# One transformer step on one core: the chunk inverse of the delta rule computed by another recurrence, in all four quarters of the array

## The reference, cut to what matters

```python
kb = kc * bc[..., None]
L = jnp.where(strict, jnp.einsum('nbhid,nbhjd->nbhij', kb, kc) * decay, 0.0)
rhs = jnp.concatenate([vc * bc[..., None], kb * jnp.exp(gc)[..., None]], axis=-1)
sol = lax.linalg.triangular_solve(eye + L, rhs, left_side=True, lower=True, unit_diagonal=True)
```

## Time and profile before

| | us |
|---|---|
| median of 3 runs | 1689.42 |
| profiled execution, whole | 1689.16 |
| its span (what the page's shares refer to) | 1687.2 |
| PE busy | 1665.5 (99%) |
| DVE busy | 1049.7 (62%) |
| ACT busy | 738.7 (44%) |
| POOL busy | 188.5 (11%) |
| part of the span in which the two inverses run | 69 to 107 and 161 to 202 |

### The profile page before, as it was taken

How to read it: one execution, slowest core, us unless ns; L and a number is a source line. 1 busy time by engine, 2 the same in 40 slices (tenths; PEclk the granted TensorE clock), 3 DMA queues, 4 the chain that set the end, 5 groups by cost and what they waited for, 6 DMA issues and landing times.

```text
span 1687.2 us, 23136 instructions
## 1 busy us (share of the span) xinstructions
PE 1665.5 (99%) x9357; PEld 1403.4 (83%) x9357; DVE 1049.7 (62%) x1567; ACT 738.7 (44%) x1137; POOL 188.5 (11%) x170
## 2 busy tenths in 40 slices
PE   9999999999999999999999999999999999999998
PEld 7787897987898888888988888888898888888887
DVE  7889798474489349549675643655574545354445
ACT  6654477553553223223542323323364645253462
POOL 0455470300300000000100000000100000000001
PEclk9999999999999999999999999999999999999999
DMA  6112134421223323323322213213212222222221
GB/s 218 60 44 63 52 106 132 139 75 51 78 73 113 102 73 118 104 78 100 119 88 81 100 51 106 100 60 110 76 66 79 72 78 86 75 88 75 87 75 51
DMA packets 45576, 147.67 MB, mean 88 GB/s; under 512 B 5024, under 2 KB 8992, under 8 KB 45472
## 3 DMA queue, kind: packets, MB, share of 16 engines
q1 hardware_dynamic: 45472, 146.21, 26.3%
HBM read 144.09 MB, written 2.10 MB: 87 GB/s over the span
## 4 chain that ended last, share of the span: by engine, by line
PE 84%; DVE 11%; ACT 2%; issue 2%; POOL 0%; DVEq 0%; ACTq 0%; POOLq 0%
PE ps L507 21%; PE ps L509 21%; PE ps L508 21%; PE ps L512 20%; DVE sl L2054 2%; DVE ps L2271 1%; DVE ps L2114 1%; DVE y L2478 1%; DVE xl L2495 1%; DVE ps L2108 0%; ACT sh L1307 0%; DVE h L2488 0%; DVE pad L2106 0%; PE ps L1128 0%; DVE ss L2232 0%
## 5 line engine op out<-in xcount | busy, mean ns | idle before, releaser
L1307 ACT ACTIVATE sh<-raw 128x1024 fp32r<-128x1024 f32 x257 | 268.2, 1053 | 372.8 <-PE ps L509 256.7
L2054 DVE TENSOR_TENSOR sl<-raw,sh 128x1024 fp32r<-128x1024 f32 x257 | 321.7, 1259 | 131.5 <-ACT sh L1307 131.4
L507 PE MATMUL ps<-xh,sh 128*128 128x512 f32 (+1 forms) x664 | 262.9, 396 | 0.0
L509 PE MATMUL ps<-xl,sh 128*128 128x512 f32 (+1 forms) x664 | 253.9, 382 | 0.0
L508 PE MATMUL ps<-xh,sl 128*128 128x512 f32 (+1 forms) x664 | 253.8, 382 | 0.0
L507 PE MATMUL ps<-sh,xh 128*128 128x512 f32 x384 | 151.8, 395 | 0.0
L509 PE MATMUL ps<-sl,xh 128*128 128x512 f32 x384 | 149.7, 390 | 0.0
L508 PE MATMUL ps<-sh,xl 128*128 128x512 f32 x384 | 149.7, 390 | 0.0
L509 PEld LDWEIGHTS ps<-xl,sh 128*128 128x128 f32 x664 | 124.8, 188 | 24.9
L507 PEld LDWEIGHTS ps<-xh,sh 128*128 128x128 f32 x664 | 124.9, 188 | 24.5 <-issue 0.7
L508 PEld LDWEIGHTS ps<-xh,sl 128*128 128x128 f32 x664 | 125.1, 188 | 22.7 <-issue 0.7
(11 more groups left out here) (438 smaller groups left out, 3320.4 us busy)
## 6 DMA issues: line engine op xcount, KB each, us to landing
raw<-in_wup SPq DMA_DIRECT2D x44, 512.0 KB, 3.5
raw<-in_wdn SPq DMA_DIRECT2D x24, 512.0 KB, 3.5
raw<-in_rqk SPq DMA_DIRECT2D x16, 512.0 KB, 3.6
raw<-in_rv SPq DMA_DIRECT2D x16, 512.0 KB, 3.4
raw<-in_rg SPq DMA_DIRECT2D x16, 512.0 KB, 4.3
raw<-in_rout SPq DMA_DIRECT2D x16, 512.0 KB, 3.5
raw<-in_sv SPq DMA_DIRECT2D x16, 512.0 KB, 3.4
raw<-in_sg SPq DMA_DIRECT2D x16, 512.0 KB, 3.5
```

Source lines behind the costliest of these rows:

```text
L507: e.matmul(dst, wh, ah, start=start, stop=False, skip_group_check=True)
L509: return e.matmul(dst, wh, al, start=False, stop=stop, skip_group_check=True)
L1307: e.activation(SH[j % NSPL][:], RAW[j % NRAW][:], ACT.Copy).then_inc(*hi(j))
L2054: e.tensor_tensor(SL[j % NSPL][:], RAW[j % NRAW][:], SH[j % NSPL][:].bitcast(F32), ALU.subtract).then_inc(*lo(j))
```

## The change

The inverse is computed by another recurrence. With L' = L plus 2I (`UL` is changed in place), D starts as L' and Z as the masked transpose (mask e1). At each of six levels there are two products: "dt" = UT^T Z, which DVE multiplies by the next mask (e2, e4, ... e32; each is half the identity minus one block pattern) to give the next Z, and "d" = Z^T UT, which ACT copies to the next `UT`. At the last level only dt is made, and DVE subtracts the identity while it writes `UTF`. So there are 1 + 5x2 + 1 = 12 products of 16 matmuls where there were 1 + 5 + 5 + 4 = 15. The POOL masks, the DVE copies L2198 and the operation `UX` are gone.

Each product now writes two banks, one per head. For head 0 of the pair a matmul goes from partitions R to the same R; for head 1 it goes to the other half (R and RO swap from level to level). Four matmuls in a row (two heads, two parities) so lie in four different 64x64 quarters. dt goes to banks 6 and 7 in both chains, d to the chain's own two. Chain 0 makes a level in one beat, so everything behind it (keys, u, w, recurrence) comes 4 beats earlier; chain 1 keeps two beats for levels 0 to 3 and one for levels 4 and 5, so its later steps stay in their beats.

The eight PSUM tensors become one of 4096 columns, of which `PS[i]` are views. The diff, cut to its core:

```diff
-CSH = ["id64", "mc", "ms", "m1t", "m2t", "m4t", "m8t", "m16t", "m32t"]
+CSH = ["id64", "mc", "ms", "e1", "e2", "e4", "e8", "e16", "e32"]
...
+        def heads(p, i):
+
+            b = 6 if i else KBANK[p][0]
+            return PSUM[:, b * 512:b * 512 + 1024].rearrange("p (h q b c) -> p h q b c", h=2, q=2, c=64)[:, :, 0]
...
# tensor_program, chain(p)
-                pe.wait_ge(*gdv[(p, "tt", 0)])
+                pe.wait_ge(*gdv[(p, "d1t")])
                 for h, tb, par in CHUNKS:
                     o = (h * 4 + tb) * 64
                     R = RR[par]
-                    t = one(b[R, o:o + 64], UTT[p][R, o:o + 64], csh["id64"][R, :], True, True)
...
-                for n_ in range(5):
...
+                    t = one(b[R, o:o + 64], UL[p][R, o:o + 64], csh["id64"][R, :], True, True)
+                t.then_inc(*gmm((p, "d", 0)))
+                rel[A_] = [(gac, (p, "d", 0))]
+                yield
+                for n_ in range(6):
+                    Z = UZ[p][n_ % 2]
+                    pe.wait_ge(*gac[(p, "d", n_)])
+                    pe.wait_ge(*gdv[(p, "z", n_)])
+                    for lhs, rhs, i in ((UT[p], Z, 1), (Z, UT[p], 0))[:2 if n_ < 5 else 1]:
+                        two = (6, 7) if i else KBANK[p]
+                        b2 = [bank(k) for k in two]
+                        for tb, h, par in product(range(NB), range(2), range(2)):
                             o = (h * 4 + tb) * 64
+                            R, RO = (RR[(par + h * m) % 2] for m in (n_, n_ + 1))
+                            t = one(b2[h][RO, tb * 64:tb * 64 + 64], lhs[R, o:o + 64], rhs[R, o:o + 64], True, True)
+                        if i:
+                            t.then_inc(*gmm((p, "dt", n_)))
+                            rel[6] = rel[7] = [(gdv, (p, "z", n_ + 1) if n_ < 5 else (p, "tt"))]
+                        else:
+                            t.then_inc(*gmm((p, "d", n_ + 1)))
+                            rel[A_] = rel[B_] = [(gac, (p, "d", n_ + 1))]
+                    yield
+                    if p and n_ < 4:
+                        yield
...
# scalar_program, chain(p)
-                ac.wait_ge(*gmm[(p, "tl")])
-                e.activation(UT[p], PS[KBANK[p][0]][:], ACT.Copy).then_inc(*gac((p, "tl", 0)))
...
+                for n_ in range(6):
+                    ac.wait_ge(*gmm[(p, "d", n_)])
+                    dst, src = (b4(UT[p]), heads(p, 0)) if n_ else (UT[p], PS[KBANK[p][0]][:])
+                    e.activation(dst, src, ACT.Copy).then_inc(*gac((p, "d", n_)))
...
# vector_program, chain(p)
-                e.scalar_tensor_tensor(g3(UTT[p]), g3(UL[p]), -1.0, bm(csh["m1t"], 8), ALU.mult, ALU.mult).then_inc(
-                    *gdv((p, "tta")))
-                ve.wait_ge(*gdv[(p, "tta")])
-                e.tensor_tensor(g3(UTT[p]), g3(UTT[p]), bm(csh["id64"], 8), ALU.add).then_inc(*gdv((p, "tt", 0)))
+                e.scalar_tensor_tensor(g3(UL[p]), bm(csh["id64"], 8), 2.0, g3(UL[p]), ALU.mult, ALU.add).then_inc(
+                    *gdv((p, "d1t")))
+                ve.wait_ge(*gdv[(p, "d1t")])
+                e.tensor_tensor(g3(UZ[p][0]), g3(UL[p]), bm(csh["e1"], 8), ALU.mult).then_inc(*gdv((p, "z", 0)))
...
+                for n_ in range(6):
+                    ve.wait_ge(*gmm[(p, "dt", n_)])
+                    if n_ < 5:
+                        e.tensor_tensor(b4(UZ[p][(n_ + 1) % 2]), heads(p, 1), bm4(csh[f"e{LEVELS[n_ + 1]}"]),
+                                        ALU.mult).then_inc(*gdv((p, "z", n_ + 1)))
+                    else:
+                        ve.wait_ge(*zero["utf"])
+                        for par in range(2):
+                            R = RR[par]
+                            t = e.tensor_tensor(UTF[R, :, R].rearrange("p (h b) c -> p h b c", h=2), heads(p, 1)[R],
+                                                bm4(csh["id64"][R, :]), ALU.subtract)
+                        t.then_inc(*gdv((p, "tt")))
...
# pool_program, chain(p): the five masks are gone
-                for n_, s in enumerate(LEVELS):
-                    po.wait_ge(*(gmm[(p, "lt", n_ - 2)] if n_ >= 2 else gdv[(p, "lt")]))
-                    e.tensor_tensor(g3(LM[p][n_ % 2]), g3(UL[p]), bm(csh[f"m{s}t"], 8), ALU.mult).then_inc(
-                        *ggp((p, "lm", n_)))
...
+                for _ in range(10):
                     yield
```

More of the change, by code:

```diff
@@ L1 @@
 from contextlib import ExitStack
+from itertools import product
 import numpy as np
@@ L179, in under @@
                 return alloc(ph, name, shape, dt)
-        PS = [root.enter_context(nc.psum_tensor(f"ps{i}", [128, 512], F32)) for i in range(8)]
+        PSUM = root.enter_context(nc.psum_tensor("ps", [128, 4096], F32))
+        PS = [PSUM[:, i * 512:i * 512 + 512] for i in range(8)]
         RAW = [alloc(root, f"raw{i}", [128, SLAB]) for i in range(NRAW)]
@@ L346, in program, with b4, bm4 @@
         UT, UX = ([R2[p][:, i * 512:i * 512 + 512] for p in range(2)] for i in range(2))
-        LM = [[R3[p][:, i * 512:i * 512 + 512] for i in range(2)] for p in range(2)]
+        UZ = [(UTT[p], UX[p]) for p in range(2)]
         KBANK = ((4, 5), (2, 3))
+        def heads(p, i):
+            b = 6 if i else KBANK[p][0]
+            return PSUM[:, b * 512:b * 512 + 1024].rearrange("p (h q b c) -> p h q b c", h=2, q=2, c=64)[:, :, 0]
+        def b4(x):
+            return x.rearrange("p (h b c) -> p h b c", h=2, c=64)
+        def bm4(x):
+            return x.unsqueeze(1).unsqueeze(1).broadcast_to([x.shape[0], 2, NB, x.shape[1]])
         WQ = [x[:].rearrange("p (g y c) -> p g y c", y=4, c=64) for x in (XWQ, UWQ)]
@@ L361, in program @@
         MSQK, RQK, NK, FJ, FK = 0, 2, 4, 5, 6
-        LEVELS = (2, 4, 8, 16, 32)
+        LEVELS = (1, 2, 4, 8, 16, 32)
         def sig(n, step=1):
@@ L726, in chain @@
                     R = RR[par]
-                    t = one(b[R, o:o + 64], UTT[p][R, o:o + 64], csh["id64"][R, :], True, True)
-                t.then_inc(*gmm((p, "tl")))
-                rel[A_] = [(gac, (p, "tl", 0))]
+                    t = one(b[R, o:o + 64], UL[p][R, o:o + 64], csh["id64"][R, :], True, True)
+                t.then_inc(*gmm((p, "d", 0)))
+                rel[A_] = [(gac, (p, "d", 0))]
                 yield
-                for n_ in range(5):
[L732 to L740, removed]
-                    yield
[L742 to L759, removed]
@@ new lines, in chain @@
+                for n_ in range(6):
[6 more added lines that the diff above has]
+                        for tb, h, par in product(range(NB), range(2), range(2)):
+                            o = (h * 4 + tb) * 64
+                            R, RO = (RR[(par + h * m) % 2] for m in (n_, n_ + 1))
[6 more added lines that the diff above has]
+                            rel[A_] = rel[B_] = [(gac, (p, "d", n_ + 1))]
+                    yield
+                    if p and n_ < 4:
+                        yield
@@ L769, in chain @@
                     b = bank(KBANK[p][h])
-                    pe.wait_ge(*gdv[(p, "tt", 5)])
+                    pe.wait_ge(*gdv[(p, "tt")])
                     pe.wait_ge(*vts[(p, h)])
@@ L1431, in chain @@
                     yield
-                ac.wait_ge(*gmm[(p, "tl")])
-                e.activation(UT[p], PS[KBANK[p][0]][:], ACT.Copy).then_inc(*gac((p, "tl", 0)))
-                yield
[L1435 to L1440, removed]
+                for n_ in range(6):
[3 more added lines that the diff above has]
+                    yield
+                    if p and 1 <= n_ < 5:
+                        yield
+                yield
                 yield
@@ L3253, in constants @@
     p, c = p % 64, c[:, :64]
-    m = {"id64": p == c, "mc": p <= c, "ms": p < c, "m1t": (p // 2 == c // 2) & (p < c)}
-    for s in (2, 4, 8, 16, 32):
-        m[f"m{s}t"] = (p // (2 * s) == c // (2 * s)) & ((c // s) % 2 == 1) & ((p // s) % 2 == 0)
+    m = {"id64": p == c, "mc": p <= c, "ms": p < c}
+    for s in (1, 2, 4, 8, 16, 32):
+        block = (p // (2 * s) == c // (2 * s)) & ((c // s) % 2 == 1) & ((p // s) % 2 == 0)
+        m[f"e{s}"] = 0.5 * (p == c) - block
     csh = np.stack([m[n].astype(np.float32) for n in CSH], 1)
```

## The result

The changed kernel takes 1672.36 us, median of 4 runs (1671.23 to 1672.97), against 1689.56 us before; the ratio is 0.9897, with a 95% interval of 0.988 to 0.9915. That is 17.2 us less. The profiled execution took 1672.97 us with a span of 1671.0.

The account below looks back on a forecast made before the run. PE was taken as the bound, with DVE nearly full behind the inverses. Savings of 10.4 and 9.8 us per chain, kept as 7.0 and 8.8, less 1 us of waits, gave 14.8 us: 1675 us, range 1670.5 to 1679.

Parts of the forecast that it names:

- PE sets the pace, products by the starts of the rows: Inverses: PE time saved there is real; fewer products and slab changes save 4.2 us per chain, 8.4 us in all.
- Quarters halve a product: Levels of both chains: four quarters save 0.46 us for each of 11 products per chain, 10.1 us in all.
- The rival without them: Levels: quarters work only two at a time, so they gain nothing; 1681.5 us, chance 0.17.
- this floor: Levels: each matmul pass costs at least some 25 ns, so a product saves about 0.12 us; 1679.5 us, chance 0.13.
- The start: Start of each chain: first product no longer waits for L2181, so it starts 1.1 and 0.5 us sooner, 1.6 us.
- Chain 0's part must pass the DVE stretch, two thirds kept: Behind chain 0's inverse DVE is nearly full, so 7.0 of chain 0's 10.4 us gain is kept.
- the 1 us charged for waits in the levels: Mainly chain 0's levels: each beat needs both results of the beat before; 1 us of new waits deducted.
- POOL and DVE relief: Per chain, DVE loses four copies, 2.7 us, and POOL 8.6 us of masks, which helps DVE's splits.
- Levels wait (slower): Levels: PE stands about 1.3 us per level for late DVE results, 16 us over twelve levels; 1697 us, chance 0.04.
- PE idle between 100 and 160 us: Sign against the forecast: this idle time grown from 4.4 us to 8 or more would mean DVE kept the time.
- the other theory: Behind the inverses: DVE gives nearly all back, PE only arrives earlier and waits; 1687.5 us, chance 0.06.
- Splits near 80 us take about 1.2 us: Sign for the forecast: with POOL's masks gone, DVE's slab splits there take about 1.2 us.

Follow-up runs that it names:

- e2: Changed kernel with the four quarters taken away in both chains (all matmuls from partitions R to the same R), two banks kept: 1681.32 us, ratio 0.9952.
- e11: Changed kernel with PE's first product (by the identity) waiting for the second DVE starting operation again: 1672.91 us, ratio 0.9902.
- e3: Changed kernel with the four quarters taken away in chain 0 alone: 1676.12 us, ratio 0.9926.
- e8: Changed kernel with four empty beats before chain 1's levels, then one beat per level, and four empty beats behind chain 0's levels: 1671.11 us, ratio 0.9887.
- e4: Changed kernel with the four quarters taken away in chain 1 alone: 1676.44 us, ratio 0.9923.
- e10: Changed kernel with the five POOL mask operations per chain put back into an unused tile: 1674.6 us, ratio 0.9911.
- e9: Changed kernel with one more DVE operation of unused result per level of chain 0, 5 in all: 1676.21 us, ratio 0.9921.
- e6: Changed kernel with chain 1 too making each level in one beat, its second beat taken out: 1669.69 us, ratio 0.9876.
- e5: Changed kernel with the same quarters in another order, all 8 matmuls of head 0, then all 8 of head 1: 1676.17 us, ratio 0.9916.
- e1: The changed kernel unaltered, measured again on the chip of the next three runs: 1673.48 us, ratio 0.9905.
- e7: Changed kernel with four empty beats before chain 1's levels, then one beat per level: 1674.9 us, ratio 0.9907.

## Why the prediction was right, and where it was off

- *PE sets the pace, products by the starts of the rows*: right. The levels take 9.2 us less PE time per chain; the sum had 4.2 + 5.1 = 9.3.
- *Quarters halve a product*: right, 0.92 to 0.47 us; 9.4 us of the time hang on them (e2). The rival without them, 1681.5 us, is close to what e2 measured, 1681.32. 32 passes in 0.51 us are 16 ns each. The Trainium skill (TensorEngine Tiling (Array Packing), Instruction Overhead) gives about 60 cycles for every matmul, by an estimate 25 ns at 2.4 GHz. The measured 16 ns are less, so this floor does not hold between quarters, and that rival falls.
- *The start*: the size was right, the reason mostly not. The waits of 1.1 and 0.5 us are gone, but e11, in which PE waits for the second operation again, loses only 0.2 us by it. That operation takes 0.69 us instead of 1.64 in chain 0, since no POOL mask runs beside it, so most of the 1.6 us came from there and not from skipping it.
- *Chain 0's part must pass the DVE stretch, two thirds kept*: this is the step that was off. It took 3.4 us from the sum; e3 shows that nine tenths of the PE time saved in chain 0 arrived, and e8 that this doesn't come from the earlier tail. What was overlooked is that DVE in the levels waits for PE's products: it enters its full stretch sooner by what PE saves, and needs no idle time to follow. With the tenth taken from chain 1 (about right: 4.6 of 5.0 us in e4) and the 1 us charged for waits in the levels (there were none in the profile after), 5.4 us were deducted from 20.2. Lost were about 2 us, since 18.1 us arrived slab by slab; PE's idle time is the same in all although 1.6 us of it had gone, so waits outside the levels grew by about as much, above all those for the keys (1.2 us) and before the last transposes of chain 0 (2.0 us, 0.4 before). That is the difference: 14.8 us forecast, 17.2 us measured, some 18 us from lowest to lowest.
- *POOL and DVE relief*: named as help and priced at nothing by itself. POOL's masks were worth about 1.1 us (e10). 3.6 us more of DVE work in chain 0's levels, for the 2.7 us that the copies had taken, cost 2.1 us of waits and then falls of the clock (e9), so the copies were probably worth less than 2.1 us of waits; no run puts back just them. DVE was nearer to setting the pace in the levels than its idle 6.1 us suggested.
- *Levels wait (slower)*: the rival needed DVE a split late; it came true once in e9 (1.3 us), when DVE had 3.6 us more to do, and once in e10 (0.7 us).
- *PE idle between 100 and 160 us*: 5.0 us (6.3 from 90 us on), under the 8 named as a sign of the other theory.
- *Splits near 80 us take about 1.2 us*: this sign did not come. The one at 79 us takes 1.70 us (2.32 before), beside an operation that POOL still has.

## What to carry to other kernels

Before you deduct for a second engine that is full further on, look at what it waits for here: DVE waited for PE, so time taken from PE came through to nine tenths. Work taken from DVE and POOL beside it counted too, and should be priced. A difference of 1 us between two runs is worth a look slab by slab: here it was one time a wait, another time a fall of the clock, and in e11 a stall that had nothing to do with the edit. Small matmuls are worth laying out over four quarters, and their order counts: neighbours in the order should lie in different quarters. An extra beat kept for safety should be tried away (e6: 2.5 to 3.8 us).

## What the runs showed of the hardware

- A further product of 16 true float32 matmuls of 64x64x64 costs PE 0.92 us with two quarters (58 ns each), 0.47 us with four (29 ns), and 0.67 us with four in a poor order (42 ns; e5: half of 1.70 less 0.36), where later matmuls of one quarter start ahead of earlier ones of another.
- The granted clock can fall to 0.50 for some 3 us behind a wait of 2.0 us in a stretch where PE was busy 3.98 of 6 us, which costs 1.2 us, and in another execution of the same kernel (e1), with the same wait of 2.0 us, it does not: 3.94 of 6 us, and 1.00 behind it:

```profile
146.00:152.00 6.00, 3.94 (x23) 2.85 (x23) 5.80 (x12) 1.68 (x4) 5.32 (x4) 1.00 0.01 1
152.50:155.50 3.00, 3.00 (x30) 2.34 (x30) 2.42 (x3) 2.61 (x3) 2.34 (x2) 1.00 0.40 153
```

- A DVE split of a slab takes 1.22 us alone and 2.21 us beside a POOL operation in e10 (2.32 us before).
- PE can stand still for 0.4 to 0.8 us in the middle of a product without a wait that the trace shows, which costs 0.7 to 1.1 us, in the same product in four of the thirteen profiled executions of kernels with the new levels (e6, e7, e10, e11).
